# A pool of weight slots with borrowed memory, and the output product and the begin of the ffn run one token tile at a time

## What is computed

```python
def first_block(x, mem, ...):
    for layer in range(2):
        h = rms_norm(x, norm_g[layer])
        proj = h @ w_in[layer]                     # queries, keys, values, gates of all heads
        o_sb  = stick_breaking_attention(...) * silu(sb_g)       # 3 pairs of heads
        o_mb  = moba_attention(rotary(...)) * silu(mb_g)         # 3 pairs of heads
        mkv   = rms_norm(mem, mem_norm_g[layer]) @ w_mem_kv[layer]
        o_mem = memory_attention(mem_q, mk, mv) * silu(mem_g)    # 4 heads
        x = x + concat(o_sb, o_mb, o_mem) @ w_out[layer]
    return rms_norm(x, final_norm_g)

def second_block(x, meta_tokens, ...):
    u = rms_norm(concat(meta_tokens, x), pre_mix_gain)
    qa, ka, va, qb, kb, vb, g = split(u @ w_in)
    o_swa  = windowed_gqa_sink_attention(rope(qa), rope(ka), va, sink)   # 4 key/value heads
    o_diff = differential_attention(rope(qb), rope(kb), vb, lam)         # 8 heads
    g_swa, g_diff = sigmoid(g + b_gate)
    merged = g_swa * (o_swa @ w_branch_swa) + g_diff * (o_diff @ w_branch_diff)
    h = x + rms_norm(merged @ w_out, post_mix_gain)
    u = rms_norm(h, pre_ffn_gain)
    f = (silu(u @ w_ffn_in[:, :D_FF]) * (u @ w_ffn_in[:, D_FF:])) @ w_ffn_out    # D_FF = 2816
    return h + rms_norm(f, post_ffn_gain)
```

## Time and profile before

| | |
|---|---|
| profiled execution | 883.49 us |
| its span, first to last instruction | 881.6 us |
| mean granted TensorE clock | 0.982 |
| TensorE matmul / weight load | 831.1 / 684.6 us |
| VectorE / ScalarE / GpSimd | 553.4 / 473.0 / 124.3 us |
| read from memory | 135.90 MB |

### The profile page before, as it was taken

How to read it: one execution, slowest core, us unless ns; L and a number is a source line. 1 busy time by engine, 2 the same in 40 slices (tenths; PEclk the granted TensorE clock), 3 DMA queues, 4 the chain that set the end, 5 groups by cost and what they waited for, 6 DMA issues and landing times.

```text
span 881.6 us, 13062 instructions
## 1 busy us (share of the span) xinstructions
PE 831.1 (94%) x4350; PEld 684.6 (78%) x4350; DVE 553.4 (63%) x857; ACT 473.0 (54%) x974; POOL 124.3 (14%) x205
## 2 busy tenths in 40 slices
PE   7998999999999999799989999999998999999996
PEld 5777877777776787689878888888886788888885
DVE  5567676676787775756555665766576555455544
ACT  5665655466775544645545566555536444344343
POOL 1110021000233210253222424200000000000000
PEclk9999999999999999899999999999999899999999
DMA  8964543366675453652212434556665556656641
GB/s 244 272 155 144 142 153 107 102 193 193 208 218 168 145 167 105 175 144 83 63 55 68 131 108 126 157 154 206 202 194 162 163 179 196 208 164 191 206 152 49
DMA packets 147456, 137.80 MB, mean 156 GB/s; under 512 B 15184, under 2 KB 115808, under 8 KB 147392
## 3 DMA queue, kind: packets, MB, share of 16 engines
q1 hardware_dynamic: 145296, 129.89, 48.8%
q0 software_dynamic: 2096, 7.09, 3.0%
HBM read 135.90 MB, written 1.05 MB: 155 GB/s over the span
## 4 chain that ended last, share of the span: by engine, by line
PE 45%; ACT 5%; DVE 3%; issue 1%; ACTq 0%; DVEq 0%
PE psum L1059 38%; PE psum L1025 3%; PE psum L1142 2%; ACT probs L1417 2%; ACT w_hi L1294 1%; PE psum L1252 1%; DVE stats L1587 1%; PE psum L1255 1%; DVE w_lo L1472 0%; ACT gtmp L1447 0%; DVE x L1505 0%; ACT p_t L1305 0%; DVE o_st L1641 0%; ACT hstat L1450 0%; DVE h_lo L1526 0%
## 5 line engine op out<-in xcount | busy, mean ns | idle before, releaser
L1472 DVE TENSOR_TENSOR w_lo<-raw,w_hi 128x1024 fp32r<-128x1024 f32 (+1 forms) x254 | 297.1, 1185 | 137.6 <-ACT w_hi L1294 78.5
L1294 ACT ACTIVATE w_hi<-raw 128x1024 fp32r<-128x1024 f32 (+1 forms) x254 | 252.8, 1015 | 65.8 <-PE psum L1059 48.6
L1059 PE MATMUL psum<-w_hi,h_hi 128*128 128x512 f32 (+1 forms) x656 | 262.6, 400 | 12.2 <-DVE h_lo L1526 11.1
L1059 PE MATMUL psum<-w_lo,h_hi 128*128 128x512 f32 (+1 forms) x656 | 248.8, 379 | 0.0
L1059 PE MATMUL psum<-w_hi,h_lo 128*128 128x512 f32 (+1 forms) x656 | 248.6, 379 | 0.0
L1059 PEld LDWEIGHTS psum<-w_hi,h_hi 128*128 128x128 f32 x656 | 125.7, 192 | 35.3 <-issue 13.5
L1059 PEld LDWEIGHTS psum<-w_lo,h_hi 128*128 128x128 f32 x656 | 125.2, 191 | 19.7
L1059 PEld LDWEIGHTS psum<-w_hi,h_lo 128*128 128x128 f32 x656 | 126.0, 192 | 16.0
L1417 ACT ACTIVATE probs<-psum,stats 128x272 f32<-128x272 f32 (+2 forms) x104 | 47.6, 467 | 87.0 <-DVE stats L1579 28.0
L1059 PE MATMUL psum<-w_hi,m_hi 128*128 128x512 f32 x152 | 60.1, 396 | 3.1 <-DVE m_lo L1526 1.7
L1059 PE MATMUL psum<-w_lo,m_hi 128*128 128x512 f32 x152 | 59.3, 390 | 0.0
(11 more groups left out here) (166 smaller groups left out, 1058.8 us busy)
## 6 DMA issues: line engine op xcount, KB each, us to landing
raw<-in_w_in SPq DMA_DIRECT2D x112, 256.0 KB, 3.5
raw<-in_w_in SPq DMA_DIRECT2D x44, 512.0 KB, 4.4
raw<-in_w_ffn_in SPq DMA_DIRECT2D x88, 256.0 KB, 3.8
raw<-in_w_out SPq DMA_DIRECT2D x24, 512.0 KB, 3.4
raw<-in_w_in SPq DMA_DIRECT2D x64, 192.0 KB, 2.7
raw<-in_w_ffn_out SPq DMA_DIRECT2D x22, 512.0 KB, 4.6
raw<-in_w_mem_kv SPq DMA_DIRECT2D x8, 512.0 KB, 3.6
raw<-in_w_branch_swa SPq DMA_DIRECT2D x8, 512.0 KB, 3.4
```

Source lines behind the costliest of these rows:

```text
L1059: last = nc.tensor.matmul(psum[:, bank, 0:n], sx[name][:, c, t * P:(t + 1) * P], wx[:, u["slot"], kk, 0:n], start=u["first"] and kk == 0 a ...
L1294: nc.scalar.activation(w_hi[:, u["slot"], :, 0:n], raw[:, u["raw"], :, 0:n], ACT.Copy)\
L1472: nc.vector.tensor_tensor(w_lo[:, u["slot"], :, 0:n], raw[:, u["raw"], :, 0:n], w_hi[:, u["slot"], :, 0:n].bitcast(F32), ALU.subtract)\
```

## The change

Slots become a pool, `free`. Two more slots lie in the memory activations `m_hi`, `m_lo` (`M_SLOTS`), from the last use of the memory product of layer 1 until the last swa group. Five more lie in memory that only attention uses (`LATE_SLOTS`), from the third gates group to the end. A slot remembers the last unit that used it (`before`); a new slot gets the last unit ahead of its entry. Splits may run six units ahead instead of three (`FAR_AHEAD`) in layer 1's `wo` and from the third gates group on. At the entry of the second block splits are held at the second swa unit (if not issued by then) until both norms are out. `wo2` runs all eight units on tile 0, then all on tile 1; ffn groups 0 and 1 do too. The outs of hidden groups 0 and 1 are taken together after group 2, those of 8 and 9 are held to the end.

```diff
 NSLOT = 5
+M_SLOTS = (5, 6)
+LATE_SLOTS = (7, 8, 9, 10, 11)
...
+FAR_AHEAD = 6
...
+    ahead = SPLIT_AHEAD
+    free, user = deque(range(NSLOT)), {}
     for what, arg in timeline:
-        if what in ("unit", "unit_a") or (what == "unit_b" and arg["g"]["kind"] == "metakv"):
+        if what == "more_slots":
+
+            for slot in arg:
+                free.appendleft(slot)
+                user[slot] = len(order) - 1
+        elif what == "fewer_slots":
+            for slot in arg:
+                free.remove(slot)
+        elif what in ("unit", "unit_a"):
+            slot = free.popleft()
+            arg["slot"], arg["before"] = slot, user.get(slot, -1)
+            user[slot] = len(order)
+            free.append(slot)
             order.append(arg)
...
-        while split < min(most, held) and split < begun + SPLIT_AHEAD and split < ended + NSLOT:
+        while split < min(most, held) and split < begun + ahead and order[split]["before"] < ended:
...
+        if layer == DEPTH - 1:
+            line.append(("ahead", FAR_AHEAD))
...
             turn_keys = memory_keys(layer + 1, {0: [after[1]], 2: norm_turns("xn", "h", 0), 3: norm_turns("xn", "h", 1)})
+            line.append(("more_slots", M_SLOTS))
...
-            line.append(after[1])
+            line.extend([("hold", None), ("ahead", SPLIT_AHEAD), after[1]])
...
+        if kv == KVH - 1:
+            line.append(("fewer_slots", M_SLOTS))
         if kv == 0:
+            line.insert(line.index(after[0]), ("hold", g["units"][1]))
...
+        if n == 2:
+            line.extend([("more_slots", LATE_SLOTS), ("ahead", FAR_AHEAD)])
...
-    line.extend(("unit", u) for u in a[:2])
+    post, pre = norm("addnorm"), norm(source="x", dest="xn")
+    turns = [norm_turns("xn", "h", t) for t in range(NT)]
+    line.extend(("unit_a", u) for u in a[:2])
     for t in range(NT):
         line.append(norm_turns("xn", "mix", t)[1])
-    line.extend(("unit", u) for u in b[:2])
-
-    post, pre = norm("addnorm"), norm(source="x", dest="xn")
-    for t, name in enumerate(("unit_a", "unit_b")):
-        for g, units in zip(wo2, (a, b)):
-            line.extend((name, u) for u in units[2:])
-            line.append(half(post, g, t))
-        if t == 0:
-            line.extend([post[0], pre[0]])
-    line.extend(norm_turns("xn", "h", 0) + [post[1]])
+    line.extend(("unit_a", u) for u in b[:2] + a[2:])
+    line.append(half(post, wo2[0], 0))
+    line.extend(("unit_a", u) for u in b[2:])
+    line.extend([half(post, wo2[1], 0), post[0], pre[0]])
+    line.extend(("unit_b", u) for u in a[:2] + b[:2] + a[2:])
+    line.append(half(post, wo2[0], 1))
+    line.append(("unit_b", b[2]))
+    line.extend(turns[0])
+    line.append(("unit_b", b[3]))
+    line.extend([half(post, wo2[1], 1), post[1], pre[1]])
...
+    line.extend(("unit_a", u) for u in f0["units"] + f1["units"][:3])
+    line.extend(turns[1])
+    line.append(("unit_a", f1["units"][3]))
+    line.extend(("unit_b", u) for u in f0["units"] + f1["units"][:2])
+    line.append(("turn_f", dict(j=0, f=f0)))
+    line.extend(("unit_b", u) for u in f1["units"][2:])
+    last_g = f1
+    for j in range(2, nf):
+        g = hidden(j, (4, 5))
+        line.extend(("unit", u) for u in g["units"][:2])
+        line.append(("turn_f", dict(j=j - 1, f=last_g)))
+        line.extend(("unit", u) for u in g["units"][2:])
+        if j < nf - 2:
+            for i in (0, 1) if j == 2 else (j - 1,):
+                line.extend(("unit", u) for u in outs_of(i))
...
-    held = outs_of(nf - 2)
+    held = outs_of(nf - 3) + outs_of(nf - 2)
...
             def split(u):
 
                 act.wait_ge(w_landed[u["raw"]], u["landed"])
-                if u["u"] >= NSLOT:
-
-                    act.wait_ge(unit_used, u["u"] - NSLOT + 1)
+                if u["before"] >= 0:
+
+                    act.wait_ge(unit_used, u["before"] + 1)
+                if u["slot"] in LATE_SLOTS:
+
+                    act.wait_ge(out_done, pl.count["outs"])
+                    act.wait_ge(out_used, pl.count["outs"])
+                    act.wait_ge(roped, pl.count["roped"])
```

More of the change, by code:

```diff
@@ L1 @@
 import math
+from collections import deque
 from contextlib import ExitStack
@@ L227, in lay_out @@
         elif what == "hold":
-            held = arg
+            held = len(order) if arg is None else order.index(arg)
+        elif what == "ahead":
+            ahead = arg
+        elif what in ("more_slots", "fewer_slots"):
+            continue
         elif what == "unit":
@@ L277, in number @@
                 s["ended"] = True
+                if s["slot"] in M_SLOTS:
+                    c0 = 4 * M_SLOTS.index(s["slot"])
+                    for c in range(c0, c0 + 4):
+                        for t in range(NT):
+                            reader[("m", c, t)] = s
             if s["last"]:
@@ L285, in number @@
             u = len(pl.units)
-            s["u"], s["slot"], s["raw"] = u, u % NSLOT, u % NRAW
+            s["u"], s["raw"] = u, u % NRAW
             slot_dmas[s["raw"]] += 16 * sum(1 if load[1] == 1 else UK for load in s["loads"])
@@ L489, in make_plan @@
             line.extend(norm_turns("xn", "h", 0))
-            line.extend([first[1], ("hold", 2), ("splits", 2)])
             mem_norm, turns = memory_norm()
             units = head_group(layer, "sb", 0)["units"]
+            line.extend([first[1], ("hold", units[2]), ("splits", 2)])
             line.append(("unit_a", units[0]))
-            line.extend(norm_turns("xn", "h", 1) + [("hold", 10 ** 6)])
+            line.extend(norm_turns("xn", "h", 1) + [("hold", None)])
             line.append(("unit_a", units[1]))
@@ L573, in make_plan, with hidden @@
     a, b = (g["units"] for g in wo2)
[L575 removed]
+    post, pre = norm("addnorm"), norm(source="x", dest="xn")
+    turns = [norm_turns("xn", "h", t) for t in range(NT)]
+    line.extend(("unit_a", u) for u in a[:2])
     for t in range(NT):
         line.append(norm_turns("xn", "mix", t)[1])
[L578 to L593 removed]
+    line.extend(("unit_a", u) for u in b[:2] + a[2:])
[8 more added lines that the diff above has]
+    line.extend([half(post, wo2[1], 1), post[1], pre[1]])
+    nf = DFF // 256
+    def hidden(j, banks):
+        return pl.group("ffn", banks, units_of(
+            lambda c: [(0, 2, W["w_ffn_in_2"], c, j * 256, DFF, 256)], "h"), j=j)
+    f0, f1 = hidden(0, (4, 5)), hidden(1, (0, 1))
     fo = [pl.group("fout", (n, 2 + n), [], n=n) for n in range(2)]
@@ L692, in build, with early, weights @@
         hstat = sb("hstat", [P, 32])
+        with ExitStack() as attention:
+            def early(name, shape):
+                return attention.enter_context(nc.sbuf_tensor(name, shape, F32))
+            stage = early("stage", [P, NSTAGE, NT, 512])
+            mkv = early("mkv", [P, NT, 2 * MEMW])
+            km_t = early("km_t", [P, 2, T])
+            sgate = early("sgate", [P, 2, NT, 256])
+            qk = early("qk", [P, 2, 784])
+            probs = early("probs", [P, 4, NT, 272])
+            sbt = early("sbt", [P, 2, 384])
+            rtmp = early("rtmp", [P, 2, 5 * DH])
+        w_hi2 = sb("w_hi2", [P, len(LATE_SLOTS), UK, 512], F32R)
+        w_lo2 = sb("w_lo2", [P, len(LATE_SLOTS), UK, 512], F32R)
+        def weights(u):
+            if u["slot"] in LATE_SLOTS:
+                n = u["slot"] - LATE_SLOTS[0]
+                return w_hi2[:, n], w_lo2[:, n]
+            if u["slot"] in M_SLOTS:
+                c = 4 * M_SLOTS.index(u["slot"])
+                return [S[:, c:c + 4, :].rearrange("p c t -> p (c t)").rearrange("p (k n) -> p k n", k=UK)
+                        for S in (S_hi["m"], S_lo["m"])]
+            return w_hi0[:, u["slot"]], w_lo0[:, u["slot"]]
         gflat = gates[:].rearrange("p t d -> p (t d)")
@@ L1041, in _ @@
                     bank = g["banks"][t]
+                    w_hi, w_lo = weights(u)
                     if g["kind"] == "metakv":
@@ L1049, in _ @@
                                 last = nc.tensor.matmul(
-                                    psum[0:3 * META, bank, 0:n], meta_s[:, c, :], wx[:, u["slot"], kk, 0:n],
+                                    psum[0:3 * META, bank, 0:n], meta_s[:, c, :], wx[:, kk, 0:n],
                                     start=u["first"] and kk == 0 and z == 0,
@@ L1059, in _ @@
                             last = nc.tensor.matmul(
-                                psum[:, bank, 0:n], sx[name][:, c, t * P:(t + 1) * P], wx[:, u["slot"], kk, 0:n],
+                                psum[:, bank, 0:n], sx[name][:, c, t * P:(t + 1) * P], wx[:, kk, 0:n],
                                 start=u["first"] and kk == 0 and z == 0, stop=u["last"] and kk == UK - 1 and z == 2,
@@ L1289, in split @@
                 act.wait_ge(w_landed[u["raw"]], u["landed"])
-                if u["u"] >= NSLOT:
-                    act.wait_ge(unit_used, u["u"] - NSLOT + 1)
+                if u["before"] >= 0:
+                    act.wait_ge(unit_used, u["before"] + 1)
```

(15 more changed lines are left out.)

26 lines of the change are left out of this document (2 added, 24 removed).

## The result

The changed kernel is slower: 900.4 us median (898.86 to 902.22), beside 885.78 for the kernel before on the same chip, a ratio of 1.0167, interval [1.0135, 1.0199]. The forecast was 895.0, slower; the time lies inside the range, 5.4 us above the forecast. The profiled execution took 902.22 us, of which 900.4 are span: 18.8 more than the span before.

The account below looks back on a forecast made before the run. TensorE was taken as the bound, busy 831.1 of 881.6 us, so only its holes and low clock could move. Gains 10.4, costs 14.6 and clock 4.5 made +8.7 on 886.5, said as 895.0; range 879 to 902.

Parts of the forecast that it names:

- First use of the M slots: Layer 1's start: splits wait for the last mkv unit, a hole of 2.4, then h_lo late; cost 3.8 us, bounds 1.0 to 4.5.
- Six ahead at layer 1's output product: Four splits issued at once delay the copy of qk, so scores start late; cost 2.8 us, bounds 0 to 4.
- First use of the late slots: Gates 2 and 3: hand-over hole 2.4 and bank add 1.7, 4.1 us; then another 3.9; bounds 2.3 to 9.
- Entry of the second block: Before the first swa matmul: only two splits left between the norms, h_lo earlier; gain 2.4 us, bounds 1.5 to 5.5.
- Output product and ffn: Second block: tile 0's norm chain lies beside seven tile units, residual wait 0.5; gain 7.8 us, bounds 5.4 to 8.3.
- End: Last hidden groups: one split goes from before m_lo; gain 0.2 us, bounds -0.5 to 0.3.
- Clock: Half clock after new holes: three of four charged, 4.5 us; bounds 0 to 11.6.
- The rival in which every hole goes cold: All four new holes followed by low clock, 11.6 us: time 902.3; chance 0.05.
- the 2.12 of the earlier trace: Wait at 460.69 in the kernel before, clock staying 1.00; taken as not following the skill's section on clock throttling.
- The term put at nothing: Every unit of 12 matmuls priced at 2.73 us, with no extra cost for those on late slots.

Follow-up runs that it names:

- e3: Changed kernel with fresh slots joining the back of the pool instead of the front; 889.03 us, ratio 1.0067 to the kernel before.
- e10: Changed kernel with edits of e2, e3, e7, three ahead at layer 1's output product, six ahead reached stepwise in second block's output product; 881.85 us, ratio 0.9993.
- e0: The changed kernel run once more with no edit, as yardstick; 899.02 us, ratio 1.0176 to the kernel before.
- e2: Changed kernel with the hold of the splits put at the second block's own norm, found by identity; 898.8 us, ratio 1.0173.
- e7: Changed kernel with the late slots 352 bytes higher in each partition; 895.81 us, ratio 1.0135.
- e11: e10 with its output product and ffn again in the order of the kernel before; 888.25 us, ratio 1.0056.
- e12: e10 with the rise moved back: four ahead from gates 2, five from gates 3, six from the product behind; 878.41 us, ratio 0.9939.

## Why the prediction was right or wrong

**First use of the M slots: right.** Forecast a hole of 2.4 on the first split and 3.8 in all; there were 2.12 and 0.61, and tile 1 started at 200.37, 3.6 us later than at 192.88 once layer 0's shift is off. The second wait is shorter than the 1.7 forecast because part of tile 0's unit before it ran at half clock (its matmuls are 0.43 us apart from 198.28 on). Behind 200.37 another 1.9 us went to the half clock that lasted to 205, where the prediction charged 1.5. e3 took the cause away and the waits went.

**Six ahead at layer 1's output product: right**, 2.8 against 2.61. Without it (e10) the trace takes 53.65 us from layer 1's last heads to the last part of its output product (288.91 to 342.56), with it (e3) 56.36 (291.57 to 347.93): 2.7.

**First use of the late slots: right, beside a cost that was not seen.** Forecast 2.4 + 1.7 + 3.9 = 8.0. The first wait is 2.56, on the high half and not the low one; the bank's 1.7 shows as 0.49, and 3.9 was 4.80. But the 0.49 is no miss. Tile 1 started at 626.93, 2.92 us behind tile 0, where a tile unit is 1.36: with the hole of 2.56 that makes 4.1, as forecast. VectorE sets it, by three splits ahead of the bank add, and TensorE at half clock (from 624.6) only waited less. In e0 the clock stayed at 1.00 there and the same two matmuls are 2.91 apart. VectorE in the changed kernel, then TensorE in e0:

```profile
622.68 3.50 DVE L1538 TENSOR_TENSOR w_lo<-raw,w_hi 128x1024 fp32r<-128x1024 f32 x3 [1.76 <-ACT w_hi L1359]
626.10 0.68 DVE L1740 TENSOR_TENSOR gates<-psum,gain 128x512 f32<-128x512 f32 x1
```
```profile
621.32 0.47 PE L1119 MATMUL psum<-w_hi,h_hi 128*128 128x512 f32 x1 [2.56 <-ACT w_hi L1359]
...
624.23 0.47 PE L1119 MATMUL psum<-w_hi,h_hi 128*128 128x512 f32 x1 [1.27 <-DVE gates L1740]
```

The stretch grew by 13.2. Of the 4.3 us beyond 4.1 and 4.80, the spacing of the matmuls gives 3.6 to the half clock behind 626.93 and from 641.6 on, and 0.7 to late-slot units at 0.234 to 0.235.

**Entry of the second block: a step that failed.** It was held that the hold would let only two splits fall between the norms. The hold never acted: `line.index(after[0])` compares by value, and the first norm of the whole program is equal to this one, so the hold went to the timeline's start, where layer 0's own hold and release undo it. The three splits of the earlier trace rows stood there again and h_lo was waited for by 4.15 us, at half clock from 368 to 379. The 1.1 us that came lie ahead of the norms, where the wait of 1.46 is gone and the clock of 0.57 at 344 was 1.00; the two were not separated. With the hold in its place (e2) the wait is the forecast 1.6, but the gain is 1.3 us and not 2.4.

**Output product and ffn: right, beside a cost that was not seen.** Forecast a residual wait of 0.5: it was 0.33, at full clock. Yet only 4.9 of the 7.8 us came. e7 shows the rest: with matching remainders, the stretch from 668.35 to 874.02 is 205.67 us, with the two tile units 208.4, against 215.85 before and 210.9 in the changed kernel. So the order is worth 7.4 us, and 2.5 of them were paid back by the late slots' slower matmuls. e11 gives 6.4 by the timing, beside waits that e10 and e11 each have of their own.

**End: right**, 1.69 to 1.50.

**Clock: a little low.** Three new cold stretches were charged with 4.5 us, and three there are, one behind the M slots and two at the gates; they took 1.9 and 3.6, 5.5 in all. The rival in which every hole goes cold, 902.3, is near the measured time, but not by its mechanism: each execution had three of the four holes cold, and not the same three. In e0 the wait of 2.54 on qk went cold and the one of 2.56 at the gates did not; in the first execution it was the other way round. The Trainium skill's page "TensorE: Matmul & The Clock Gate", section "HAM oscillation — how this bites in real kernels", says that a TensorE that keeps idling starts its work throttled; in its example the waits are of about 3 to 5 us. The new hole of 4.80 follows that. The shorter ones are outside the example: 2.56 went cold in the first execution, and the hole of 2.1 at the diff heads again stayed warm in the changed kernel and went cold in e0 (466 to 471). So the 2.12 of the earlier trace rows is no case against the section.

**The term put at nothing: the matmuls on the late slots.** The prediction gave a unit 2.73 us whatever slot it lies in. Late-slot units cost 0.7 us more up to 672.83 and 2.5 behind it. These 3.2 us are half of the 6.3 by which the stretches without layer 0 exceed the +8.7; e7, which takes only this away, is 3.6 us under e0 by the ratios. The rest is the entry (1.3 less gained), the hole of 4.80 (0.9) and the clock (1.0), with smaller ones of both signs. So the direction was no luck; nearly all misses have one sign, and the time lies inside the range because the range was wide.

## What to carry to other kernels

A borrowed buffer should enter a pool at the back: at the front, its first user waits for the last reader of the borrowed memory, and an in-order queue makes everything behind it wait too (here 9.6 us). More run-ahead isn't free where the same queue also empties banks: the wait for it was 6.07 us when it was raised at once (e3), 3.08 beside the norms (e10), and 0.76 when it was raised by one per group, away from norms (e12). What the late slots are worth with three ahead, no run shows. A stretch at half clock costs nothing where the engine would wait behind it anyway. Look in the trace for each step that an edit puts into a list, and at the remainders of the starts of a matmul's two operands when new buffers are laid out.

## What the runs showed of the hardware

A chain of 72 matmuls of 512 columns takes 16.36 us or up to 16.81, by the layout alone, with no wait in it: 0.2267 us a matmul where the starts of the weight slots and of the activations' tensors in a partition leave the same remainder to 4096 bytes, more where they don't. Fast pairs seen: 384 with 384, 2560 with 2560, 736 with 736. Slow ones, weights first, in us a matmul: 32 with 384 (0.2333 to 0.2350), 64 with 384 (0.2333), 384 with 2560 (0.2305 to 0.2333), 384 with 736 (0.2333 to 0.2350). What decides must be finer than 4096: inside a slot the operands of a matmul lie 2048 bytes apart, inside the activations 512, so those of a fast pair agree only to 512 bytes. And the slow pair 384 with 2560 differs by 17 x 128. If it is a power of two that must divide the difference, 256 and 512 are left; that is worked out from the layouts and was not tried, nor what inside the chip does it. The Trainium skill's page "SBUF — State Buffer", section "SBUF: two separate sides", says that TensorE's port never waits on another engine. Nothing here speaks against that, since the order of work was the same in all these runs; it doesn't name what two operands of TensorE's own do to each other, and that is what the runs show.
